# A two-block layer kernel on one core: decay rows of the gated delta rule by one product and a broadcast through DRAM, instead of eight groups of products

## The reference, cut to what matters

```python
def gdn_mixer(x, w_in, conv_w, a_log, dt_bias, norm_w, w_out):
    p = x @ w_in
    qkv = causal_conv_silu(p[..., :GDN_QKV], conv_w)
    ...
    beta = jax.nn.sigmoid(b_logit)
    g = -jnp.exp(a_log.astype(f32)) * jax.nn.softplus(a_logit + dt_bias.astype(f32))
    o = gated_delta_rule(q, k, v, g, beta)

def gated_delta_rule(q, k, v, g, beta):
    ...
    gc = jnp.cumsum(g, axis=-1)
    diff = gc[..., :, None] - gc[..., None, :]
    decay = jnp.where(causal, jnp.exp(jnp.where(causal, diff, 0.0)), 0.0)
    kb = k * beta
    A = jnp.where(strict, jnp.einsum('bhncd,bhnsd->bhncs', kb, k) * decay, 0.0)
    ...
```

## Time and profile before

| | us |
|---|---|
| median of 3 executions | 1169.47 (1168.94 to 1169.72) |
| the profiled execution's own time | 1169.41 |
| its span in the profile | 1167.6 |
| TensorE busy | 1148.7 (98%) |
| VectorE busy | 557.3 (48%) |
| ScalarE busy | 500.0 (43%) |
| GpSimd busy | 442.0 (38%) |
| DMA, mean over the span | 109 GB/s |

### The profile page before, as it was taken

One profiled execution on the slowest core, in us unless ns is written; L12 is line 12 of the kernel. 1 busy time (PEld: TensorE's weight loads), 2 busy tenths in 40 slices (PEclk: granted clock), 3 DMA queues, 4 the chain that ended last, 5 costly groups with the idle time before them and its releaser, 6 DMA issues.

```text
span 1167.6 us, 18001 instructions
## 1 busy us (share of the span) xinstructions
PE 1148.7 (98%) x7288; PEld 944.5 (81%) x7288; DVE 557.3 (48%) x891; ACT 500.0 (43%) x663; POOL 442.0 (38%) x336
## 2 busy tenths in 40 slices
PE   9899999999999999999999999999999999999997
PEld 7568888888888888888788788888888888888886
DVE  2572554334541154556883447622210344576835
ACT  4474553543421135774443324564421344544531
POOL 0105554544544551434431311024445525455420
PEclk9999999999999999999999999999999999999999
DMA  9994232233243243223242213013242422323201
GB/s 348 384 384 142 72 108 95 85 108 101 78 129 108 75 142 109 73 72 109 73 110 73 73 37 109 1 37 96 85 156 79 138 77 72 109 74 102 81 1 73
DMA packets 104314, 127.77 MB, mean 109 GB/s; under 512 B 13251, under 2 KB 90801, under 8 KB 104117
## 3 DMA queue, kind: packets, MB, share of 16 engines
q1 hardware_dynamic: 99138, 119.62, 31.2%
q10 hardware_dynamic: 5107, 7.16, 1.8%
HBM read 121.53 MB, written 5.24 MB: 109 GB/s over the span
## 4 chain that ended last, share of the span: by engine, by line
PE 92%; DVE 4%; ACT 2%; DMA 1%; issue 1%; SPq 0%; POOL 0%; DVEq 0%; ACTq 0%; POOLq 0%
PE ps L273 25%; PE ps L275 24%; PE ps L274 24%; PE ps L1709 3%; PE ps L1735 1%; PE ps L2185 1%; PE ps L2266 1%; DMA ada<-in_ada_w 1%; PE ps L2272 1%; PE ps L1715 1%; PE ps L2267 1%; DVE conv_v L1235 1%; PE ps L1778 1%; PE ps L2248 1%; PE ps L1986 1%
## 5 line engine op out<-in xcount | busy, mean ns | idle before, releaser
L407 POOL TENSOR_TENSOR wl<-raw,wh 128x512 fp32r<-128x512 f32 x312 | 420.8, 1381 | 645.2 <-ACT wh L444 645.2
L273 PE MATMUL ps<-xth,wh 128*128 128x512 f32 (+1 forms) x832 | 325.7, 391 | 0.8 <-DVE xtl L1132 0.6
L275 PE MATMUL ps<-xth,wl 128*128 128x512 f32 (+1 forms) x832 | 317.6, 382 | 0.0
L274 PE MATMUL ps<-xtl,wh 128*128 128x512 f32 (+1 forms) x832 | 317.3, 381 | 0.0
L444 ACT ACTIVATE wh<-raw 128x2048 fp32r<-128x2048 f32 x78 | 149.3, 1913 | 298.9 <-PE ps L275 279.4
L273 PEld LDWEIGHTS ps<-xth,wh 128*128 128x128 f32 x832 | 156.5, 188 | 34.5 <-issue 4.8
L275 PEld LDWEIGHTS ps<-xth,wl 128*128 128x128 f32 x832 | 156.4, 188 | 30.7
L274 PEld LDWEIGHTS ps<-xtl,wh 128*128 128x128 f32 x832 | 156.7, 188 | 28.3 <-issue 0.5
L1140 DVE SCALAR_TENSOR_TENSOR conv_out<-ps,conv_taps,conv_out 128x511 f32<-128x511 f32 x44 | 32.7, 744 | 122.6 <-ACT conv_out L609 122.6
L1235 DVE SCALAR_TENSOR_TENSOR conv_v<-ps,gdn_taps,conv_v 128x511 f32<-128x511 f32 (+2 forms) x96 | 71.8, 748 | 35.7 <-ACT conv_v L677 32.9
L273 PE MATMUL ps<-wh,xth 128*128 128x512 f32 x176 | 69.7, 396 | 0.1
(11 more groups left out here) (342 smaller groups left out, 1671.9 us busy)
## 6 DMA issues: line engine op xcount, KB each, us to landing
ada<-in_ada_w SPq DMA_DIRECT2D x24, 1024.0 KB, 10.7
raw<-in_gdn_w_in SPq DMA_DIRECT2D x24, 1024.0 KB, 5.2
raw<-in_ffn_w_up SPq DMA_DIRECT2D x22, 1024.0 KB, 4.9
raw<-in_gla_w_in SPq DMA_DIRECT2D x12, 1024.0 KB, 5.0
raw<-in_ffn_w_down SPq DMA_DIRECT2D x11, 1024.0 KB, 4.9
raw<-in_gdn_w_out SPq DMA_DIRECT2D x8, 1024.0 KB, 4.9
raw<-in_gla_w_out SPq DMA_DIRECT2D x4, 1024.0 KB, 4.9
xres<-in_x SPq DMA_DIRECT2D x4, 512.0 KB, 5.0
```

Source lines behind the costliest of these rows:

```text
L273: nc.tensor.matmul(o, lh, rh, start=first, stop=False)
L274: nc.tensor.matmul(o, lh, rl, start=False, stop=False)
L275: return nc.tensor.matmul(o, ll, rh, start=False, stop=last)
L407: rest = nc.gpsimd.tensor_tensor(lo[:, part], raw[:, s, part], hi[:, part].bitcast(f32), ALU.subtract)
```

## The change

The decay rows are no longer made by products. One more product in `gate_sums` has GLOG as the stationary side and `tri` as the moving one: it gives all 32 rows (4 chunks, 8 heads) at once, on 32 partitions, in bank 7, columns 128 to 255. ScalarE copies them to `gc_turned`, issues a DMA to a scratch tensor in DRAM, waits for it, and issues two DMAs that read the scratch back with every partition getting the same 16 rows (8 KB each, 1 MB in all per DMA), straight into `attn`. `dec(c)` then works in place in `attn`, waits for the broadcast of its half, and both its tensor inputs are in SBUF. Its calls are placed otherwise between the taps. `turn_sums(0)` moves from the end of piece (2,1) to ahead of k = 2 in piece (3,0). `keys_keys` 0 to 2 need not wait for VectorE to read the banks. Small steps of the gate logits use the helper `step` instead of another semaphore.

```diff
@@ build @@
+    gc_turned = at("gc_turned", TMP + 14 * KB + 512, [P])
+    gc_rows = nc.dram_tensor("gc_rows", (TT * H, P), f32).ap()
+        gc_read = [S("gc_read0"), S("gc_read1")]
@@ scalar @@
             silu(0, 0)
+            act.wait_ge(S("gc_mm"), 1)
+            nc.scalar.activation(gc_turned[0:TT * H, :], ps[0:TT * H, 7, 128:256], ACT.Copy).then_inc(S("gc_turned"), 1)
+            act.wait_ge(S("gc_turned"), 1)
+            act.dma_start(gc_rows, gc_turned[0:TT * H, :]).then_inc(S("gc_written"), 16)
             conv_first(0, 1)
             high_gin(2)
+            act.wait_ge(S("gc_written"), 16)
+            for half in range(2):
+                q = slice(half * TT * H // 2, (half + 1) * TT * H // 2)
+                act.dma_start(attn[:, 2 * half:2 * half + 2].rearrange("p t h c -> p (t h c)"),
+                              gc_rows[q, :].rearrange("q c -> (q c)").partition_broadcast(P)).then_inc(gc_read[half], 16)
             silu(0, 1)
@@ vector @@
             def dec(c):
 
                 i, g = c // 2, c % 2
-                v.wait_ge(S("gcrow_mm"), c + 1)
+                v.wait_ge(gc_read[i // 2], 16)
                 for h in range(4 * g, 4 * g + 4):
-                    dd = V.scalar_tensor_tensor(attn[:, i, h, :], ps[:, cell_bank(c), (h % 4) * P:(h % 4 + 1) * P], scal[:, GC, i, h:h + 1],
+                    dd = V.scalar_tensor_tensor(attn[:, i, h, :], attn[:, i, h, :], scal[:, GC, i, h:h + 1],
                                                 mask_add[:], ALU.subtract, ALU.min)
                 dd.then_inc(S("dec_diff"), 1)
...
             dec(0)
+            taps(1, 1)
             dec(1)
-            taps(1, 1)
             dec(2)
+            taps(2, 0)
             dec(3)
-            taps(2, 0)
-            dec(4)
-            dec(5)
             taps(2, 1)
             key_sums(0)
-            dec(6)
-            dec(7)
+            for c in range(4, 8):
+                dec(c)
@@ tensor @@
             def keys_keys(c):
 
                 i, g = cell(c)
-                if c < 3:
-                    pe.wait_ge(S("dec_diff"), c + 6)
-                else:
+                if c == 0:
+                    pe.wait_ge(S("gc_exp"), 3)
+                elif c >= 3:
                     pe.wait_ge(S("neg_done"), c - 2)
...
-                X.matmul(ps[:, 7, 96:128], ones[:, 0:1].broadcast_to([P, P]), glog, start=True, stop=True).then_inc(S("gc_mm"), 1)
+                X.matmul(ps[:, 7, 96:128], ones[:, 0:1].broadcast_to([P, P]), glog, start=True, stop=True)
+                X.matmul(ps[0:TT * H, 7, 128:256], glog, tri[:], start=True, stop=True).then_inc(S("gc_mm"), 1)
 
             chunk(1, 0, (3, gate_sums))
-            chunk(1, 1, (3, do(gc_row, 0)), (6, do(gc_row, 1)))
-            chunk(2, 0, (3, do(gc_row, 2)), (6, do(gc_row, 3)))
-            chunk(2, 1, (3, do(gc_row, 4)), (4, do(sums, 0)), (6, do(gc_row, 5)), end=[do(turn_sums, 0)])
-            chunk(3, 0, (3, do(gc_row, 6)), (6, do(gc_row, 7)))
+            chunk(1, 1)
+            chunk(2, 0)
+            chunk(2, 1, (4, do(sums, 0)))
+            chunk(3, 0, (2, do(turn_sums, 0)))
```

More of the change, by code:

```diff
@@ L1352, in _ @@
             v.wait_ge(S("alog_in"), 48)
-            V.tensor_tensor(ba_tmp[:, 1], ba[:, :, H:2 * H], alog_dt[:, 1, :].unsqueeze(1).broadcast_to([P, TT, H]), ALU.add)\
-                .then_inc(S("ba_z"), 1)
-            V.tensor_copy(ba_tmp[:, 0], ba[:, :, 0:H]).then_inc(S("ba_z"), 1)
-            v.wait_ge(S("ba_z"), 2)
+            step(V.tensor_tensor(ba_tmp[:, 1], ba[:, :, H:2 * H], alog_dt[:, 1, :].unsqueeze(1).broadcast_to([P, TT, H]), ALU.add))
+            step(V.tensor_copy(ba_tmp[:, 0], ba[:, :, 0:H]))
             V.scalar_tensor_tensor(ba_tmp[:, 2], ba_tmp[:, 1], -1.0, ba_tmp[:, 1], ALU.mult, ALU.min).then_inc(S("ba_ready"), 1)
@@ L1359, in _ @@
             v.wait_ge(S("ba_exp"), 5)
-            V.tensor_scalar(ba_tmp[:, 0], ba_tmp[:, 0], 1.0, None, ALU.add).then_inc(S("ba_z"), 1)
-            V.scalar_tensor_tensor(ba_tmp[:, 3], ba_tmp[:, 1], 0.0, ba_tmp[:, 2], ALU.max, ALU.add).then_inc(S("ba_z"), 1)
-            v.wait_ge(S("ba_z"), 4)
+            step(V.tensor_scalar(ba_tmp[:, 0], ba_tmp[:, 0], 1.0, None, ALU.add))
+            step(V.scalar_tensor_tensor(ba_tmp[:, 3], ba_tmp[:, 1], 0.0, ba_tmp[:, 2], ALU.max, ALU.add))
             V.reciprocal(ba_tmp[:, 0], ba_tmp[:, 0]).then_inc(S("gates_ready"), 1)
@@ L2048, in turn_sums @@
                 mm.then_inc(S("ss_mm"), 1)
-            def gc_row(c):
-                i, g = c // 2, c % 2
-                if c == 2:
-                    pe.wait_ge(S("gc_exp"), 3)
-                if c >= 3:
-                    pe.wait_ge(S("dec_diff"), c - 2)
-                for h in range(4 * g, 4 * g + 4):
-                    mm = X.matmul(ps[:, cell_bank(c), (h % 4) * P:(h % 4 + 1) * P], scal[:, GLOG, i, h:h + 1].broadcast_to([P, P]), tri[:],
-                                  start=True, stop=True)
-                mm.then_inc(S("gcrow_mm"), 1)
             def keys_keys(c):
                 i, g = cell(c)
-                if c < 3:
-                    pe.wait_ge(S("dec_diff"), c + 6)
-                else:
+                if c == 0:
+                    pe.wait_ge(S("gc_exp"), 3)
+                elif c >= 3:
                     pe.wait_ge(S("neg_done"), c - 2)
```

## The result

| | before | changed |
|---|---|---|
| median of 8 executions each, us | 1169.68 (1168.94 to 1171.25) | 1173.21 (1171.67 to 1174.34) |
| granted clock, mean of the profiled execution | 0.997 | 0.993 |

The ratio is 1.0028, 95% interval 1.0018 to 1.0039: the changed kernel is **slower by 0.28%**, where 0.4% faster was forecast. The profiled execution took 1173.83 us, its span is 1172.0. The eight executions of the changed kernel fall into two groups by their mean granted clock: four at 0.995 took 1171.67 to 1172.95 us, four at 0.993, the profiled one among them, 1173.47 to 1174.34. In the profiled one the clock of the first 30 us, where the code is the same, was lower than before (0.89 against 0.94), which is worth about 1.5 us. So part of the 3.5 us between the medians is probably not the change's; what follows counts from the traces.

A forecast was written before the change was run, and what follows sets the result against it. TensorE, busy 98% of the span, was taken as the bound; -7.12 + 0.22 + 1.0 + 0.8 + 0.2 = -4.9, +0.4 for issues, gave -4.5 us: 1165.0 us, range 1163.7 to 1172.4.

The forecast's parts named there:

- VectorE waits once and then holds: Decay steps beside GpSimd's splits of units 3 and 4: VectorE waits for one quarter, then keeps GpSimd off.
- sums(1): TensorE at sums(1) waits 0.2 us for ScalarE's square(3).
- Removed and added on TensorE: Eight gc_row calls go, -7.12 us; one fp32 product of 128 columns comes, +0.22 us.
- The DMA part: ScalarE's issues 0.35 to 1.16 us each; write landed 2.7 us after issue; broadcasts take 6 and 9 us.
- +0.4 for slow issues: Added to the sum of -4.9 us for ScalarE's DMA issues between 0.35 and 1.16 us.
- Where they meet: Decay steps behind taps(n,1) ask 0.4 us into GpSimd's split: dec(1), dec(2) at unit 3, dec(4) to dec(7) at unit 4.
- Waits for GpSimd's splits: TensorE waits 1.0 us for unit 3 at chunk (3,0) and 0.8 us for unit 4 at chunk (4,0).
- Turning and keys_keys(3): The sum had no wait at the turning in chunk (3,0) or at keys_keys(3).
- Behind that no order changes: After sums(1) every engine stands to TensorE as before, so the shift should stay to the end.
- Rival D: Decay steps beside GpSimd's splits: every instruction takes turns with a quarter; +2.6 us, 1172.0, with slow issues 1174.6; chance 0.24.
- The slow end of A: Forecast case, VectorE waits once and holds, 1164.5 to 1167.2 us, chance 0.52; its slow end has issues of 1.16 us.

The follow-up runs named there:

- experiment 4: Changed kernel with decay steps regrouped or GpSimd's split start moved; with one row of 32: 1168.01 us, and 1169.84 us with the split released by VectorE's count.
- the first kernel of experiment 4: Changed kernel with all eight decay steps in one row of 32 instructions behind the taps of (1,0): 1168.01 us.
- experiment 3: Changed kernel with 18 unused products of 128 columns on TensorE ahead of sums(1): 1169.83 us, ratio 0.9999 to the kernel before.

## Why the prediction was wrong

The step that failed: **"VectorE waits once and then holds."** The runs showed turns instead, one VectorE instruction per quarter of GpSimd's, rows of 6.00 and 8.00 us and a wait of 4.4 us at sums(1) where 0.2 was forecast. The step was chosen because opcode, form and spacing of a decay step are those of the row at 139.20. What decided was none of these. The row there had run 4.1 us when GpSimd asked at 139.20, as VectorE's timeline of the kernel before has it,

```profile
135.10 6.42 DVE L1179 SCALAR_TENSOR_TENSOR g_acc<-ada,c_col,g_acc 128x256 f32<-128x256 f32 x16
```

while the decay steps began after GpSimd had. Holding is real, also for decay steps (quarters of 2.12 to 4.65 us where 1.26 is usual), but in these runs only for a row that had run 2.3 us or more when GpSimd asked; one of 1.2 us took turns. That GpSimd would come first at both splits stood in the prediction's own working (split from 481.15, dec(1) at 481.6), and was not weighed against the place it took as its model.

Point by point:

- *Removed and added on TensorE* (-7.12, +0.22): right in sum, since without collisions -6.56 came, where -6.4 is their sum with one wait; the one product alone cost 0.44, not a fourth of a group of four.
- *The DMA part*: right, and cheaper. Issues 0.34 and 0.83 us for two; the table of DMAs of the changed kernel (KB each, us from issue to landing) has

```profile
gc_rows<-gc_turned ACTq DMA_DIRECT2D x1, 16.0 KB, 1.4
...
attn<-gc_rows ACTq DMA_DIRECT2D x2, 1024.0 KB, 5.7
```

  where 2.7, and 6 and 9, were taken (5.7 is the middle of 4.7 and 6.7). The +0.4 for slow issues was not needed; dec(0) waited for nothing.
- *Where they meet*: right, 0.4 and 0.5 us into the splits of units 3 and 4.
- *Waits for GpSimd's splits* (1.0 and 0.8): neither came, because GpSimd was never held.
- *sums(1)* (+0.2): 4.4. *Turning and keys_keys(3)* (0 in the forecast): 0.6 and 1.4.
- *Behind that no order changes*: right.
- *TensorE's clock*: no term of the sum or of a rival had it. It cost 2.8 us behind the wait at sums(1).

Rival D, at 0.24, was the case that came, by its mechanism (one instruction per quarter) and its places. Of its three waits the square at sums(1) was 4.8 forecast and 4.4 measured; the turning 2.25 and 0.6, keys_keys(3) 2.5 and 1.4. Less the 1.46 us of shift, taps(2,0) began 1.1 us and taps(3,0), behind the key factors, 2.2 us earlier than D had them. Of this, 0.9 us per split is the length of a turn: D added VectorE's instruction to the quarter, 1.26 + 0.27 = 1.53 us, while the split with its turns lasted 5.18, or 1.30 a turn. Its own sum was too high by 3.1 in the waits and had nothing for the clock, 2.8 us; that the two errors nearly cancelled, at 1172.0 against 1173.21, is luck. The range ended 0.8 us below the result, at 1172.4, which it calls the middle of D; between D's own 1172.0 and 1174.6 the middle is 1173.3. The slow end of A counts its issues twice as well (-4.9 + 0.6 + 1.7 is -2.6, or 1166.8, not 1167.2), which changes no conclusion.

The Trainium skill, "SBUF — State Buffer", section "Who interferes with whom", calls the shared port pair an exclusive lock, held for the whole instruction by whoever issues first. Taken with the lock freed after each instruction, this gave D. The change agrees with it (1.37 us for an instruction of 0.34). The places where a row held a quarter for up to 3.4 us do not: there GpSimd stood still over as many as thirteen instructions.

## What to carry to other kernels

Count the SBUF inputs of each VectorE instruction before and after a change. Moving one operand from PSUM to SBUF left the instruction as fast as before (1.13 us for four) where GpSimd was idle or only wrote, and made the two rows beside a split 3.8 and 3.7 us longer, which ate the 6.9 us that the removed products gave. Where such a row must run beside a reader on GpSimd, put one operand in PSUM or move the row; cutting GpSimd's work finer, or making it wait, returned little. And where a wait of several us on TensorE is forecast, add what the products behind it cost at the lower clock: here that, 2.8 us, was the difference between no change and slower.

## What was not expected of the hardware

- Whether VectorE and GpSimd took turns or VectorE held went with how long VectorE's gapless row had run when GpSimd asked: turns at 1.2 us, held at 2.3 and more, in seven kernels.
- TensorE's lower clock (1.2 of 2.4 GHz) came with each long wait seen: 4.4 us in the change, 3.7 us with the rows of 32 in experiment 4, 3.3 us at the late split of unit 4. The windows of the first kernel of experiment 4 are

```profile
486.00:488.00 2.00, 0.00 (x0) 0.00 (x0) 0.68 (x1) 1.25 (x2) 2.00 (x2) 1.00 0.00 0
488.00:490.00 2.00, 1.51 (x9) 0.25 (x9) 0.92 (x2) 1.01 (x2) 1.27 (x2) 0.75 0.00 0
490.00:492.00 2.00, 2.00 (x5) 1.62 (x6) 1.32 (x2) 0.60 (x2) 0.00 (x0) 0.50 0.70 172
```

  Products put into the wait, in experiment 3, kept it at 1.00.
- Two DMAs, issued 0.4 us apart, that each give all 128 partitions the same 8 KB from DRAM (1 MB) landed in 4.7 and 6.7 us, where the 1 MB weight load takes 5.2, and the 16 KB before them in 1.4.
